# Swapping the second and third matmul of each tile in the three-product units of a hybrid decoder step

## The reference, cut to what matters

```python
proj = h @ p['w_in']                       # its first columns here: the RWKV part
mixed = sigmoid(ga) * (o_a @ p['w_pa']) + sigmoid(gb) * (o_b @ p['w_pb'])
x = x + mixed @ p['w_o']
h2 = _rmsnorm(x, p['g_ffn'])
x = x + (silu(h2 @ p['w_gate']) * (h2 @ p['w_up'])) @ p['w_down']
```

## Time and profile before

| | before |
|---|---|
| median of 3 runs | 2046.54 us (2039.28 to 2046.58) |
| the profiled execution | 2043.91 us, its span 2042.1 us |
| PE, PEld busy | 1995.0 us, 1802.9 us |
| DVE, ACT, POOL busy | 1064.3 us, 732.6 us, 44.5 us |
| bytes moved | 378.13 MB, 185 GB/s |

### The profile page before, as it was taken

The page is one execution under the profiler, slowest core; times in us unless marked ns, Lnnn a source line. Parts: engine busy times, 40 slices in busy tenths (PEclk is TensorE's granted clock), DMA queues, the critical chain, the costliest instruction groups (busy, mean ns, idle before and its releaser), DMA issues.

```text
span 2042.1 us, 38026 instructions
## 1 busy us (share of the span) xinstructions
PE 1995.0 (98%) x15613; PEld 1802.9 (88%) x15613; DVE 1064.3 (52%) x1272; ACT 732.6 (36%) x964; POOL 44.5 (2%) x63
## 2 busy tenths in 40 slices
PE   8999989999999999999999999999999999999996
PEld 7999766678875766699999999999999999999996
DVE  6655966378873520154445555444555555444444
ACT  6333101432233110144444444444444444333332
POOL 0000002200000000000000000000000000000000
PEclk9999998999999999999999999999999999999998
DMA  6444257344558898834446554444444444544443
GB/s 263 174 155 158 103 196 173 89 141 132 174 194 292 280 385 341 330 125 165 163 165 222 188 175 165 166 165 166 167 167 168 167 168 152 200 159 168 161 164 117
DMA packets 103625, 378.13 MB, mean 185 GB/s; under 512 B 26995, under 2 KB 36851, under 8 KB 76147
## 3 DMA queue, kind: packets, MB, share of 16 engines
q1 hardware_dynamic: 78802, 346.88, 48.6%
q0 software_dynamic: 4736, 18.80, 2.8%
q10 hardware_dynamic: 20000, 11.28, 2.0%
HBM read 359.30 MB, written 17.58 MB: 185 GB/s over the span
## 4 chain that ended last, share of the span: by engine, by line
PE 89%; DVE 4%; SPq 3%; DMA 2%; issue 1%; ACT 1%; DVEq 0%; ACTq 0%
PE ps L466 15%; PE ps L1075 14%; PE ps L1076 14%; PE ps L1077 13%; PE ps L1030 5%; PE ps L1032 5%; PE ps L1031 5%; PE ps L499 2%; PE ps L498 2%; PE ps L500 2%; PE ps L986 1%; PE ps L937 1%; SPq L359 1%; SPq L360 1%; PE ps L510 1%
## 5 line engine op out<-in xcount | busy, mean ns | idle before, releaser
L2003 DVE TENSOR_TENSOR weights_lo<-ring,weights_hi 128x2048 fp32r<-128x2048 f32 (+1 forms) x152 | 305.6, 2011 | 284.8 <-ACT weights_hi L1515 284.8
L1076 PE MATMUL ps<-h_lo,weights_hi 128*128 128x288 f32 x1408 | 416.1, 296 | 0.0
L1075 PE MATMUL ps<-h_hi,weights_hi 128*128 128x288 f32 x1408 | 414.6, 294 | 0.3 <-DVE weights_lo L2003 0.3
L1077 PE MATMUL ps<-h_hi,weights_lo 128*128 128x288 f32 x1408 | 412.5, 293 | 0.0
L1515 ACT ACTIVATE weights_hi<-ring 128x2048 fp32r<-128x2048 f32 (+1 forms) x152 | 257.1, 1691 | 365.9 <-PE ps L1077 356.8
L466 PE MATMUL ps<-hT,ring 128*128 128x288 f32 x1472 | 387.6, 416 | 0.0
L466 PEld LDWEIGHTS ps<-hT,ring 128*128 128x128 f32 x1472 | 276.7, 193 | 80.2 <-issue 7.1
L1077 PEld LDWEIGHTS ps<-h_hi,weights_lo 128*128 128x128 f32 x1408 | 265.1, 188 | 0.0
L1075 PEld LDWEIGHTS ps<-h_hi,weights_hi 128*128 128x128 f32 x1408 | 264.1, 188 | 0.6 <-DVE weights_lo L2003 0.6
L1076 PEld LDWEIGHTS ps<-h_lo,weights_hi 128*128 128x128 f32 x1408 | 264.4, 188 | 0.1
L1075 PE MATMUL ps<-act_hi,weights_hi 128*128 128x288 f32 x704 | 208.4, 296 | 0.0
(11 more groups left out here) (356 smaller groups left out, 2979.9 us busy)
## 6 DMA issues: line engine op xcount, KB each, us to landing
ring<-in_wst SPq DMA_DIRECT2D x209, 1024.0 KB, 4.9
ring<-in_wdn SPq DMA_DIRECT2D x64, 704.0 KB, 4.1
arena<-in_v SPq DMA_DIRECT2D x64, 512.0 KB, 5.5
arena<-in_kT SPq DMA_DIRECT2D x112, 256.0 KB, 5.6
arena<-chunk_ar_bk ACTq DMA_DIRECT2D x24, 256.0 KB, 3.9
arena<-in_ki SPq DMA_DIRECT2D x64, 64.0 KB, 1.9
arena<-in_kT SPq DMA_DIRECT2D x8, 512.0 KB, 6.5
arena<-in_xT SPq DMA_DIRECT2D x4, 592.0 KB, 6.7
```

Of the source, the lines that this page charges most:

```text
L1075: mm(out, W_HI[:, (u - U_FF) % 2, w], hi, start=start, stop=False)
L1076: mm(out, W_HI[:, (u - U_FF) % 2, w], lo, start=False, stop=False)
L1077: return mm(out, W_LO[:, u % 4, w], hi, start=False, stop=stop)
L2003: tt(W_LO[:, u % 4, 0:m], raw, W_HI[:, at, 0:m].bitcast(F32), ALU.subtract).then_inc(sem("w_split"), 1)
```

## The change

In the three inner bodies the second and the third matmul change places. Afterwards a tile is: high weights with high tokens, low weights with high tokens, high weights with low tokens. The `stop` flag and the `unit_read` count go with the last place.

```diff
@@ first_unit
                     mm(out, W_HI1[:, (u0 + s) % 2, w], H_HI1[:, k, :], start=(k == 0), stop=False)
-                    mm(out, W_HI1[:, (u0 + s) % 2, w], H_LO1[:, k, :], start=False, stop=False)
-                    ins = mm(out, W_LO[:, slot, w], H_HI1[:, k, :], start=False, stop=(k == KT - 1))
+                    mm(out, W_LO[:, slot, w], H_HI1[:, k, :], start=False, stop=False)
+                    ins = mm(out, W_HI1[:, (u0 + s) % 2, w], H_LO1[:, k, :], start=False, stop=(k == KT - 1))
@@ mix_three
                 mm(out, MW_HI[:, (u - U_MIX) % 2, w], hi, start=start, stop=False)
-                mm(out, MW_HI[:, (u - U_MIX) % 2, w], lo, start=False, stop=False)
-                return mm(out, W_LO[:, u % 4, w], hi, start=False, stop=stop)
+                mm(out, W_LO[:, u % 4, w], hi, start=False, stop=False)
+                return mm(out, MW_HI[:, (u - U_MIX) % 2, w], lo, start=False, stop=stop)
@@ three
                 mm(out, W_HI[:, (u - U_FF) % 2, w], hi, start=start, stop=False)
-                mm(out, W_HI[:, (u - U_FF) % 2, w], lo, start=False, stop=False)
-                return mm(out, W_LO[:, u % 4, w], hi, start=False, stop=stop)
+                mm(out, W_LO[:, u % 4, w], hi, start=False, stop=False)
+                return mm(out, W_HI[:, (u - U_FF) % 2, w], lo, start=False, stop=stop)
```

## The result

The changed kernel takes 2046.77 us (median of 20 runs, 2043.74 to 2051.72), the kernel before 2040.12 us (median of 20 runs, 2036.94 to 2048.36). The ratio is 1.003, with a 95% interval of 1.0022 to 1.0038: slower by 0.3%, some 6 us. That is inside the 0.5% that I had set as what can be told from no change, but 20 runs of each do tell it. The forecast of no change was wrong; its rival B, in the slower direction, is what happened.

A forecast was written before the change was run, and what follows sets the result against it. PE's matmul spacing times the number of tiles was taken as the bound; all terms summed to 0 us against the profiled 2043.9 us, and with the runs' median 2.6 us higher the forecast was 2045 us, range 2036 to 2053.

The forecast's parts named there:

- forecast of no change: Whole kernel: no change beyond 2 us, chance 0.65; predicted time 2045 us.
- rival B: The 1664 mixed-pitch tiles go to 400 ns (+5.7 us, about 2051) or towards 390 (down to 2034); chance 0.23.
- What bounds the kernel: Three-product stages: only the spacing of PE's own matmuls sets the time, multiplied by the number of tiles.
- Instructions, waits, clock: Changed stages: no instruction added or removed, no new wait, granted clock still 1.00; 0 us each.
- Neighbours: Each tile exchanges one same-weights step for one same-tokens step between successive matmuls; taken as 0 us.
- keeping the weights saves nothing: First loop at 136.7 ns a matmul against 136 with all operands changing: losing the same-weights step costs nothing.
- same-tokens step: Two successive matmuls of a tile reading the same tokens: taken as 0, gain bounded at 40 us.
- Layout: 1664 gate, up and mixing tiles with pitches 296 and 288: taken as 0, bounds +5.7 and -11.0 us.
- absolute level: Whole kernel: 2045 us, set between the profiled execution's 2043.9 and the median of the runs shown, 2.6 us higher.
- share of 1600 tiles at 0 us: First loop, attention and RWKV outputs, output and down units: one pitch for both halves, same address sequence in both orders, 0 us.

The follow-up runs named there:

- four orders side by side: Kernel before, gate, up and down units given four product orders in turn: 399.4, 399.2, 395.6, 395.8 ns a gate and up tile; 400.0 ns a down tile.
- first sweep: Kernel before, both pitches 288, gate and up high tokens shifted 32 to 128 bytes by blocks of four tiles, down low tokens 160: down tile 393.3 ns.

## Why the prediction was wrong

- *What bounds the kernel* was right: PE's spacing times the number of tiles gives 5.7 us, inside the 4.5 to 7.8 us of the timed runs.
- *Instructions, waits, clock* at 0 us were right: in the changed stages the counts, the waits and the granted clock of 1.00 are unchanged. The three waits that are missing after lie elsewhere.
- *Neighbours*: "keeping the weights saves nothing" and 0 for the same-tokens step were right. The down, output and first-loop tiles stayed at 400.0, 400.0 and 409.1 ns, and in the down units all of the four orders side by side took 400.0.
- *Layout* is the step that failed. I had its place, its 1664 tiles and its upper bound of +5.7 us, and then took 0, "since the reason for the 3.4 ns is that the two pitches are mixed, and they stay so". That treated the gain of the mixed pitch as a property of the layout. It is one of layout and order together: 4.2 ns a tile below the 400.0 of equal placement in the old order, 0.8 in the new. It came to +5.7 us by the trace. That this is the bound itself is luck: the bound compared 396.6 ns, which has the pauses at the loop turns in it, with 400.0, which has none. Without them the gain was 4.2 ns, and losing all of it would have been 4.2 x 1664 = 7.0 us; the new order kept 0.8 ns a tile of it. Where an edit changes the sequence of addresses and the trace shows that addresses matter, "it stays" is a guess with no better claim than the bound; and since the old value was known to be the favourable one, below the plain 400.0 of every other stage, the odds were on a loss. B had 0.23 and should have had most of the weight on its slow side.
- The *absolute level* was taken from three runs of before with a median of 2046.5; 20 runs have 2040.1. The predicted 2045 lies 2 us from what was measured for the changed kernel, but only because these two errors cancel.
- The term's *share of 1600 tiles at 0 us* held, but its reason, that "high and low of one tile stand alike", is too weak: the shifted down units have one pitch too, and there the order is worth 7.8 ns a tile. In the kernel before, all these halves lie a whole number of 256 bytes apart.
- No placement that was timed more than once is clearly faster than the kernel before; the best, with both down halves moved, is at 0.9995 with an interval that holds 1.

## What to carry to other kernels

When a stream of matmuls runs without idle time, compare the time of a tile between stages of the same shape before changing anything: a difference of a per cent with equal clock and equal counts pointed here to where the operands lie. An exchange of two neighbours, a pitch, or a shift of a buffer each moved it by up to 2%, so an edit is not neutral by being "only an order" unless the operands lie alike. Don't read the price of a placement from single tiles or short blocks: patterns run over several tiles, and have to be measured in a steady stage, behind the stage that will really run ahead of it. And work out by how much an edit moves a buffer before building an argument on the move.

## What the runs showed of the hardware

- The start-to-start distance of float32r matmuls of 288 columns at the upper clock depends on where the successive token tiles and the weights lie: averaged over their repeats, tiles of three took from 387.5 ns (a shifted tile of the first sweep) to 408.3 (with the weights moved), and most stages lay between 393 and 401. With one pitch of 288 columns and a whole number of 256 bytes between the halves, it is 400.0 in every order that was run.
- With mixed pitch the tile times repeat every eight tiles, as the distance between the halves does modulo 256 bytes.
- All operands moved together by 13056 bytes, 51 x 256: no change. Tokens moved by 256 bytes against the weights: no change (398.3 and 398.3). Weights moved by 128 bytes: a change in both stages.
- One placement showed three patterns (398.3 on the mean; 389.2 and 397.5 in turn; a round of 390.0, 396.7, 394.2 and 392.5), each kept over the 704 tiles of the stage but for the first few.
- A second product with the same weights has a full weight load of its own, 188 ns, and brings no gain; nor does a second product with the same tokens (400.0 ns a down tile in all four orders).
